# MLA scores in five single-pass products with rounded parts, and a rearranged opening

## The chip, the cores and the metric

The kernel runs on one core of a Trainium2 chip. The time is the device time of one execution, in microseconds; lower is better. The median of three runs of the kernel before is 2233.78 us (2233.66 to 2234.05).

## What is computed

Four layers on x of 512 tokens by 1024 features in float32. Layers 0 and 3 mix tokens by multi-head latent attention (MLA), layer 1 by a recurrent block, layer 2 by sliding-window attention; each layer then has a squared-ReLU MLP of width 4096, and a norm ends it. The change touches the MLA layers and the opening:

```python
def _mla(h, positions, w_in, q_norm, kv_norm, w_uq, w_ukv, w_o):
    c_q, c_kv, k_rope = jnp.split(h @ w_in, [384, 640], axis=-1)
    q = (_rmsnorm(c_q, q_norm) @ w_uq).reshape(B, S, 8, 128 + 64)
    q_nope, q_rope = q[..., :128], _rope(q[..., 128:], positions, 64)
    kv = (_rmsnorm(c_kv, kv_norm) @ w_ukv).reshape(B, S, 8, 128 + 128)
    k_nope, v = kv[..., :128], kv[..., 128:]
    k_rope = _rope(k_rope[:, :, None, :], positions, 64)[:, :, 0, :]
    for s0 in range(0, S, 128):       # block b of 128 queries sees 128 * (b + 1) keys
        s = (q_nope . k_nope + q_rope . k_rope) * (128 + 64) ** -0.5
        p = softmax(where(chunk_id[q] >= chunk_id[k], s, -1e30))
        o = p @ v
    return o @ w_o
```

## The kernel before

**Layout and weights.** Everything lies with features on the partitions and tokens along the free axis, in chunks of 128 features by 512 tokens. Weights stream through four slots (`w_raw`) in units of mostly 512 KB, in the order of `weight_units`. For each unit ScalarE makes the rounded high part (`w_hi`, `split`, L1622) and VectorE the rest (`w_lo`, L981). A projection is three single-pass products in the type float32r (`product`, L503 to L505): high by high, high by low, low by high. `square_group` (L511) takes four units of 512 by 512 columns into four PSUM banks. PSUM is used as four areas of two banks each; an area is claimed by TensorE and freed by its reader, by a semaphore that counts.

**Order.** Each engine has its program written out by hand, in the same order of tasks, with waits on semaphores. Nothing reorders them. SyncE issues all weight loads; a slot is reloaded when its low part has been made.

**The opening.** SyncE issues the column constants, then in turn 512 KB of x (two chunks) and a weight unit, four times. For each pair of chunks ScalarE makes the high parts of x times the norm's gain (L1639) and the squares (L1651), then the high part of the unit; VectorE follows with the low parts (L999, L981). GpSimd first computes the rotary angles of all tokens (`angles`, L2020 to L2062, some forty small operations of 128 by 128), and after them adds the squares (L2011).

**An MLA layer** (`mla`: L622 on TensorE, L1156 on VectorE, L1743 on ScalarE). Four units give the query compression and a part of the rest; before the third of them stand the two products that spread the angles (`rotary_angles`, L587, L588), of which ScalarE makes sin and cos (L1736, L1737), and before the fourth the token sums of squares (L564). Two narrow tail units follow. A norm goes through small columns: token sums, a root on ScalarE (L1665), Newton steps and a diagonal on VectorE (`norm_columns`, L1041), and a product of the diagonal with ones that spreads the scale over the partitions (L576, `spread`).

Then come two halves of four heads. A half starts with a projection stage: queries of two pairs of heads, keys and values of two pairs. VectorE multiplies nope queries (L1186), rotary queries (L1190) and keys (L1200) by their token scales out of PSUM, rotates with the help of a product with a permutation (L620, L1139 to L1142) and writes the values (L1206). Then attention takes the heads one after another: scores (two fp32 products for each block of queries, L704 with 128 rows and L706 with 64, key widths 512, 384, 256 and 128), mask (L1219), negated maximum (L1223), Exp with its sum (L1781), reciprocal and scaling of p (L1237, L1240), ten transposes (L720), their copies (ScalarE L1790, VectorE L1234), the weighted sum of values (L732), and its high and low parts (L1741, L1154). TensorE's order in a turn is scores of head i, weighted sum of head i - 2, transposes of head i - 1:

```python
for i in range(HALF_HEADS + 1):
    if i < HALF_HEADS: scores(i)
    if i >= 2: weighted(i - 2)
    if i >= 1 and (half, i) != (1, HALF_HEADS): transposes(i - 1)
```

Of the kernel before, what the change touches and what calls it, by code (L numbers as in the profile page):

```python
# [22 lines left out]
ALU = mybir.AluOpType  # L23
# [202 lines left out]
def trunk(nc, A):  # L226
# [3 lines left out]
    with ExitStack() as ctx:  # L230
# [23 lines left out]
        arena = sb("arena", [P, ARENA])  # L254

        def cut(*sizes):

            out, at = {}, 0
            for name, n in sizes:
# [6 lines left out]
        mla_m = cut(("qn", 4 * T), ("qr", 2 * T), ("kn", 4 * T), ("kr", T), ("v", 4 * T), ("rq", T), ("rkv", T),  # L266
                    ("pt", ATT), ("p", 2 * ATT))
# [19 lines left out]
        rstd2_4 = small[:, 64:68]  # L287
        diag = var
# [27 lines left out]
        x_loaded = [sem(f"x_loaded{i}") for i in range(4)]  # L316
        cols_loaded = sem("cols_loaded")
# [30 lines left out]
        o_hi_done = sem("o_hi_done")  # L348
        y_done = sem("y_done")
# [22 lines left out]
        OHI, OLO = HI[4:] + UHI[4:], LO[4:] + ULO[4:]  # L372
# [23 lines left out]
        def _(sp):  # L396
# [53 lines left out]
            for p in range(4):  # L450
# [34 lines left out]
        def _(pe):  # L485
# [24 lines left out]

            def square_group(areas, hi, lo, ready, before_unit=None):  # L511
# [3 lines left out]
                for kp in range(4):  # L515
# [63 lines left out]
            def rotary_angles(which):  # L579

                def run():
                    claim(3)
# [4 lines left out]
                    nc.tensor.matmul(bank(3, 0), pick, tab_m["wide_sin"], start=True, stop=True)  # L587
                    nc.tensor.matmul(bank(3, 1), pick, tab_m["wide_cos"], start=True, stop=True  # L588
# [33 lines left out]
            def mla(j):  # L622
                square_group((0, 1), HI, LO, h_chunks, {2: rotary_angles(0), 3: token_sums(2, ssq, 7)})
# [4 lines left out]
                for kq in range(2):  # L628
# [32 lines left out]
                def keys(a):  # L661
                    next_unit_ready()
                    claim(a)
                    wh, wl = (w.rearrange("p (k h n) -> p k h n", k=2, h=2) for w in unit())
# [20 lines left out]
                def swap(a, source, claimed=True):  # L685
                    if not claimed:
                        claim(a)
                    c.add("rows")
                    pe.wait_ge(rows_ready, c.now("rows"))
                    swap_rows(bank(a, 1), 0, source).then_inc(psum_done, 1)  # L690
                    c.add("psum_done")

                qn, kn, qr, kr, v = (mla_m[n] for n in ("qn", "kn", "qr", "kr", "v"))

                def scores(i):
                    rows = slice(ROPE * (i % 2), ROPE * (i % 2) + ROPE)
# [52 lines left out]
                for half in range(2):  # L749
# [3 lines left out]
                    if half == 0:  # L753
                        swap(2, mla_m["kr"], claimed=False)
                        token_sums(3, mla_m["rkv"], 1)()
                    queries((2, 3))
                    swap(1, chunk(mla_m["qr"], 0))
                    if half == 0:
                        spread(1, claimed=True)
                    keys(0)  # L760
                    if half == 1:
                        pe.wait_ge(area_free[4], c.at("area4"))
                    swap(3, chunk(mla_m["qr"], 1))
                    values(1)
                    keys(2)
# [190 lines left out]
        def _(dve):  # L956
# [67 lines left out]
            def norm_columns(out, a, n, inner=False, scale=1.0):  # L1024
# [13 lines left out]
                if inner:  # L1038
                    link(nc.vector.tensor_tensor(out, out, rstd4, ALU.mult))
                dve.wait_ge(const_loaded, 32)  # L1040
# [11 lines left out]
            def tables_made():  # L1052

                c.add("psum_done")
                c.add("area3")
                return c.now("area3")
# [99 lines left out]
            def mla(j, gain):  # L1156
                split(3)
                tables = tables_made()
# [18 lines left out]
                norm_columns(token_scale, 2, QL, inner=True, scale=SCALE)  # L1177
# [954 lines left out]
```

## Time and profile before

| what | us |
|---|---|
| median of three runs | 2233.78 |
| the profiled execution, its own time | 2234.83 |
| its span in the trace | 2233.1 |
| TensorE busy | 2147.3 (96%) |
| VectorE, ScalarE, GpSimd busy | 1163.4, 760.3, 180.5 |
| mean granted TensorE clock | 0.978 |

PE is TensorE, PEld its weight loads, DVE VectorE, ACT ScalarE, POOL GpSimd. The length of a matmul in the trace is that of its way through the array; matmuls overlap, and what one costs in a row of many is the distance of the starts. An fp32 product shows as two instructions (x2). A granted clock of 1.00 stands for 2.4 GHz, 0.50 for 1.2 GHz. In brackets behind an instruction is the idle time of its engine before it, and what ended that.

### The profile page before, as it was taken

How to read it: one execution, taken by the hardware profiler on the slowest of the kernel's cores; microseconds unless marked ns; L12 is line 12 of the kernel's file. 1: busy time of each engine (PE TensorE's matmuls, PEld its weight loads, DVE VectorE, ACT ScalarE, POOL GpSimd, SP SyncE). 2: the span in 40 equal slices, each digit the busy share in tenths (PEclk: the TensorE clock that was granted, in tenths of full speed). 3: DMA queues.
4: the chain of work that ended last, by engine and by line, in shares of the span. 5: the costliest groups of instructions: out<-in, count | busy, mean ns of one | idle time of the engine just before them, and what ended most of it. 6: DMA issues, size and time to landing. Idle time of an engine off the chain costs nothing.

```text
span 2233.1 us, 24820 instructions
## 1 busy us (share of the span) xinstructions
PE 2147.3 (96%) x9774; PEld 1716.7 (77%) x9774; DVE 1163.4 (52%) x1341; ACT 760.3 (34%) x1063; POOL 180.5 (8%) x199
## 2 busy tenths in 40 slices
PE   5999999999998999999997899999999999999997
PEld 4665888888876888888885788888876668888886
DVE  3653554444679654444566464344466537344444
ACT  4222432232456432232334442322342234232231
POOL 5000100000110200003110010000420001000000
PEclk8998999999999999999998899999999999999998
DMA  5200322233222322322321122322232012323221
GB/s 153 68 19 20 104 94 95 94 100 98 85 85 66 111 97 97 100 94 95 101 81 48 38 95 95 99 99 94 96 97 68 31 35 86 104 94 99 98 94 38
DMA packets 113134, 187.97 MB, mean 84 GB/s; under 512 B 14880, under 2 KB 26016, under 8 KB 113056
## 3 DMA queue, kind: packets, MB, share of 16 engines
q1 hardware_dynamic: 112720, 186.83, 26.0%
q8 instruction: 53, 0.87, 0.2%
q14 instruction: 25, 0.20, 0.0%
q10 hardware_dynamic: 336, 0.07, 0.0%
HBM read 184.78 MB, written 2.10 MB: 84 GB/s over the span
## 4 chain that ended last, share of the span: by engine, by line
PE 91%; DVE 5%; ACT 3%; POOL 1%; issue 1%; DMA 0%; ACTq 0%; DVEq 0%; POOLq 0%
PE psum L503 27%; PE psum L505 27%; PE psum L504 27%; PE psum L706 2%; PE psum L704 2%; PE psum L732 2%; PE psum L720 1%; PE psum L620 1%; ACT arena L1962 0%; PE psum L576 0%; DVE small L1529 0%; ACT w_hi L1622 0%; DMA const_sb<-in_const 0%; PE psum L880 0%; DVE w_lo L981 0%
## 5 line engine op out<-in xcount | busy, mean ns | idle before, releaser
L981 DVE TENSOR_TENSOR w_lo<-w_raw,w_hi 128x1024 fp32r<-128x1024 f32 (+1 forms) x346 | 428.2, 1243 | 821.5 <-ACT w_hi L1622 820.8
L1622 ACT ACTIVATE w_hi<-w_raw 128x1024 fp32r<-128x1024 f32 (+1 forms) x346 | 365.3, 1060 | 1087.8 <-PE psum L505 1087.7
L503 PE MATMUL psum<-h_hi,w_hi 128*128 128x512 f32 x1392 | 551.1, 396 | 17.2 <-DVE w_lo L981 17.2
L504 PE MATMUL psum<-h_lo,w_hi 128*128 128x512 f32 x1392 | 543.6, 391 | 0.0
L505 PE MATMUL psum<-h_hi,w_lo 128*128 128x512 f32 x1392 | 543.6, 390 | 0.0
L503 PE MATMUL psum<-u_hi,w_hi 128*128 128x512 f32 x1336 | 525.9, 394 | 7.5 <-ACT arena L1842 7.3
L504 PE MATMUL psum<-u_lo,w_hi 128*128 128x512 f32 x1336 | 521.8, 391 | 0.0
L505 PE MATMUL psum<-u_hi,w_lo 128*128 128x512 f32 x1336 | 521.6, 390 | 0.0
L503 PEld LDWEIGHTS psum<-h_hi,w_hi 128*128 128x128 f32 x1392 | 262.7, 189 | 75.0 <-issue 15.7
L504 PEld LDWEIGHTS psum<-h_lo,w_hi 128*128 128x128 f32 x1392 | 262.6, 189 | 57.4 <-issue 3.6
L505 PEld LDWEIGHTS psum<-h_hi,w_lo 128*128 128x128 f32 x1392 | 262.4, 188 | 55.2
L503 PEld LDWEIGHTS psum<-u_hi,w_hi 128*128 128x128 f32 x1336 | 252.1, 189 | 61.8 <-ACT arena L1842 8.1
L504 PEld LDWEIGHTS psum<-u_lo,w_hi 128*128 128x128 f32 x1336 | 252.2, 189 | 53.2 <-issue 1.4
L505 PEld LDWEIGHTS psum<-u_hi,w_lo 128*128 128x128 f32 x1336 | 251.9, 189 | 52.9
L2011 POOL TENSOR_TENSOR ssq<-ssq,sq 128x512 f32<-128x512 f32 x52 | 82.0, 1576 | 1353.5 <-ACT sq L1651 1351.2
L999 DVE SCALAR_TENSOR_TENSOR h_lo<-x,cols_sb,h_hi 128x512 fp32r<-128x512 f32 x64 | 86.7, 1406 | 10.4 <-ACT h_hi L1639 10.4
L1081 DVE TENSOR_TENSOR arena<-psum,rstd 128x1024 f32<-128x1024 f32 x64 | 78.0, 1218 | 13.8 <-PE psum L505 13.8
L1685 ACT ACTIVATE u_hi<-arena 128x1024 fp32r<-128x1024 f32 x64 | 68.0, 1062 | 34.8 <-DVE arena L1064 32.5
L1084 DVE TENSOR_TENSOR x<-x,arena 128x1024 f32<-128x1024 f32 x64 | 78.4, 1225 | 2.2
L1064 DVE TENSOR_TENSOR arena<-arena 128x1024 f32<-128x1024 f32 x64 | 76.1, 1230 | 0.0
L1068 DVE TENSOR_TENSOR u_lo<-arena,u_hi 128x1024 fp32r<-128x1024 f32 x64 | 75.9, 1228 | 0.0
L704 PE MATMUL psum<-arena 128*128 128x512 f32 (+3 forms) x128 | 56.4, 525 | 8.5 <-DVE arena L1206 5.3
(190 smaller groups left out, 1323.8 us busy)
## 6 DMA issues: line engine op xcount, KB each, us to landing
w_raw<-in_mlp_w SPq DMA_DIRECT2D x256, 512.0 KB, 3.7
w_raw<-in_mla_w_o SPq DMA_DIRECT2D x16, 512.0 KB, 3.5
w_raw<-in_lru_w_in SPq DMA_DIRECT2D x16, 512.0 KB, 3.9
w_raw<-in_swa_w_in SPq DMA_DIRECT2D x12, 512.0 KB, 3.7
w_raw<-in_mla_w_in SPq DMA_DIRECT2D x8, 512.0 KB, 4.7
w_raw<-in_mla_w_ukv SPq DMA_DIRECT2D x8, 512.0 KB, 4.5
w_raw<-in_lru_w_out SPq DMA_DIRECT2D x8, 512.0 KB, 3.4
w_raw<-in_swa_w_o SPq DMA_DIRECT2D x8, 512.0 KB, 3.4
```

What stands on the lines that cost most here:

```text
L503: nc.tensor.matmul(out, stat[0], mov[0], start=start, stop=False, skip_group_check=skip)
L504: nc.tensor.matmul(out, stat[0], mov[1], start=False, stop=False, skip_group_check=skip)
L505: return nc.tensor.matmul(out, stat[1], mov[0], start=False, stop=stop, skip_group_check=skip)
L704: nc.tensor.matmul(out, chunk(qn, i)[:, q_at], chunk(kn, i)[:, 0:keys_n], start=True, stop=False)
L981: nc.vector.tensor_tensor(w_lo[:, to], w_raw[:, to], exact(w_hi[:, to]), ALU.subtract).then_inc(w_ready, 1)
L999: nc.vector.scalar_tensor_tensor(out=LO[k], in0=chunk(x, k), scalar=col(*gain(k)), in1=exact(HI[k]), op0=ALU.mult, op1=ALU.subtract).then_ ...
L1064: nc.vector.tensor_tensor(r, r, r, ALU.mult).then_inc(squared, 1)
L1068: nc.vector.tensor_tensor(chunk(u_lo, 2 * (a + q), 2), chunk(mlp_m["relu"], 2 * q, 2), exact(chunk(u_hi, 2 * (a + q), 2)), ALU.subtract).t ...
L1081: free(nc.vector.tensor_tensor(two(chunk(mlp_m["scaled"], 2 * q, 2)), two(area(a)), twice(rstd2[:, :]), ALU.mult), a)
L1084: nc.vector.tensor_tensor(chunk(x, 2 * a, 2), chunk(x, 2 * a, 2), chunk(mlp_m["scaled"], 2 * q, 2), ALU.add).then_inc(x_ready, 1)
L1622: nc.scalar.activation(w_hi[:, to], w_raw[:, to], ACT.Copy).then_inc(w_hi_done, 1)
L2011: g.tensor_tensor(to, to, source, ALU.add).then_inc(squares_added, 1)
```

## The change

1. *Scores.* The nope queries are no longer multiplied by their token scale. ScalarE writes their high part (`query_hi`), VectorE the low part (`query_lo`). Keys are scaled into `k_wide`, then cut into high and low (`key_hi`, `key_lo`). Each rotated head is stored as 64 rows of high part and 64 rows of low part in one tile (`ROPE_Q`), and the rotary key has its high and low parts on 128 rows. A block of scores is five float32r products in place of two fp32 ones. The query's scale (`q_scale`) is applied by Exp and, for the maximum, by one small multiplication per area; its diagonal product is gone.
2. *First loads.* x and weights of the first unit come in halves of 256 KB, with semaphores of their own, and `first_unit` takes their products in the order in which the parts become ready. A small Square on ScalarE stands ahead.
3. *Squares.* Those of the opening are made by ScalarE behind each unit's high part and added by VectorE.
4. *Rotary angles.* Their products stand ahead of the last chunk of the second tail unit, in area 2; sin and cos are made after the second root. The frequency columns are loaded ahead of the positions.

```diff
 # TensorE
+            def first_unit(outs):
+                for kk in range(2):
+                    at = [slice(kk * T + m * P, kk * T + (m + 1) * P) for m in range(4)]
+                    pe.wait_ge(h_hi_done, kk + 1)
...
+                    for m in range(4):
+                        nc.tensor.matmul(outs[m], w_hi[:, at[m]], HI[kk], start=kk == 0, stop=False)
+                    pe.wait_ge(h_ready, kk + 1)
+                    for m in range(4):
+                        nc.tensor.matmul(outs[m], w_hi[:, at[m]], LO[kk], start=False, stop=False)
...
-                square_group((0, 1), HI, LO, h_chunks, {2: rotary_angles(0), 3: token_sums(2, ssq, 7)})
+                square_group((0, 1), HI, LO, h_chunks, {3: token_sums(2, ssq, 7)})
...
+                        if k == KC - 1:
+                            rotary_angles(0, 2)()
...
-                spread(2)
...
-                            nc.tensor.matmul(out, chunk(qn, i)[:, q_at], chunk(kn, i)[:, 0:keys_n],
-                                             start=True, stop=False)
-                            mm = nc.tensor.matmul(out, chunk(qr, i // 2)[rows, q_at], kr[rows, 0:keys_n],
+                            nc.tensor.matmul(out, qh, KHI[i][:, 0:keys_n], start=True, stop=False)
+                            nc.tensor.matmul(out, qh, KLO[i][:, 0:keys_n], start=False, stop=False)
+                            nc.tensor.matmul(out, ql, KHI[i][:, 0:keys_n], start=False, stop=False)
+                            nc.tensor.matmul(out, ROPE_Q[i][:, q_at], ROPE_KHI[:, 0:keys_n], start=False, stop=False)
+                            mm = nc.tensor.matmul(out, ROPE_Q[i][:, q_at], ROPE_KLO[:, 0:keys_n],
                                                   start=False, stop=True)
 # VectorE, the areas' maxima
+                                link(ins)
...
+                                nc.vector.tensor_tensor(lows, lows, q_scale[:, first:first + 2], ALU.mult
+                                                        ).then_inc(nmax_ready, 1)
 # VectorE, projection stage
-                    nope_queries(0, 0)
-                    units_passed(1)
-                    rotary_queries(0, 1)
+                    query_lo(0, 0)
...
+                        nc.vector.tensor_tensor(ROPE_KLO, k_raw, exact(ROPE_KHI), ALU.subtract)
...
                     finish(0, 1, wait=half == 1)
                     keys(0, 0)
+                    rope_lo(0)
                     finish(1, 3)
+                    key_lo(0)
                     values(0, 1)
+                    rope_lo(1)
                     keys(1, 2)
                     values(1, 3)
+                    key_lo(1)
                     split(2)
                     attention(half)
 # ScalarE, a half
-                    split(4)
...
+                    sum_ready()
+                    query_hi(0, 0)
+                    query_rope(0, 1)
                     if half == 1:
+                        head_hi(OHI[HALF_HEADS - 1])
+                    split(1)
+                    if half == 0:
...
+                        nc.scalar.activation(ROPE_KHI, k_raw, ACT.Copy).then_inc(rope_hi_done, 1)
+                        column_root()
+                    sum_ready()
+                    query_hi(1, 2)
+                    query_rope(1, 3)
+                    split(1)
...
+                    rope_hi(0)
...
+                    key_hi(0, half)
...
+                    rope_hi(1)
+                    c.add("tensor_unit")
+                    split(1)
...
+                    key_hi(1, half)
+                    c.add("tensor_unit")
+                    split(1)
                     attention(half)
```

## Rows read from the trace of the kernel before

**Rows 1.** The page, busy time of TensorE and its weight loads.

```profile
PE 2147.3 (96%) x9774; PEld 1716.7 (77%) x9774; DVE 1163.4 (52%) x1341; ACT 760.3 (34%) x1063; POOL 180.5 (8%) x199
```

**Rows 2.** Waits of PE, 0 to 170 us: engine, line, releaser, total, times, longest.

```profile
PE psum L587 <- POOL arena L2062: 11.6, 1, 11.6
...
PE psum L576 <- DVE var L1041: 0.8, 1, 0.8
```

**Rows 3.** Timeline of the opening: start, length, engine, line, operation, idle before.

```profile
6.05 1.28 ACT L1639 ACT_TABLE_LOAD   x1 [6.05 <-DMA x<-in_x]
...
12.11 0.76 PE L503 MATMUL psum<-h_hi,w_hi 128*128 128x512 f32 x1 [12.11 <-DVE w_lo L981]
...
15.58 0.40 PE L503 MATMUL psum<-h_hi,w_hi 128*128 128x512 f32 x1
...
24.22 0.39 PE L505 MATMUL psum<-h_hi,w_lo 128*128 128x512 f32 x1
```

**Rows 4.** Timeline, the angles on POOL and the matmul behind them.

```profile
21.82 1.15 POOL L2033 TENSOR_SCALAR arena<-arena 128x128 f32<-128x128 f32 x1
...
24.89 0.30 POOL L2033 TENSOR_SCALAR arena<-arena 128x128 f32<-128x128 f32 x1
...
36.26 1.19 PE L587 MATMUL psum<-arena,const_sb 128*128 128x512 f32 x1 [11.65 <-POOL arena L2062]
```

**Rows 5.** Windows: stretch, length, busy per engine, granted clock (PEclk), DMA.

```profile
36.30:42.30 6.00, 6.00 (x10) 3.41 (x11) 0.00 (x0) 0.00 (x0) 5.69 (x5) 0.50 0.00 0
```

**Rows 6.** Timeline of PE, a head of MLA layer 2 and the end of its half.

```profile
1739.36 1.02 PE L704 MATMUL psum<-arena 128*128 128x512 f32 x2
...
1744.31 0.49 PE L704 MATMUL psum<-arena 128*128 128x128 f32 x2
...
1745.14 2.42 PE L732 MATMUL psum<-arena 128*128 128x512 f32 x8
1747.40 1.25 PE L720 MATMUL psum<-const_sb,arena 128*128 128x128 f32 x10
...
1752.73 0.48 PE L503 MATMUL psum<-u_hi,w_hi 128*128 128x512 f32 x1
```

**Rows 7.** Timeline of PE, two single-pass matmuls of 256 columns.

```profile
1771.99 0.28 PE L505 MATMUL psum<-w_hi,u_lo 128*128 128x256 f32 x1
1772.11 0.28 PE L503 MATMUL psum<-w_hi,u_hi 128*128 128x256 f32 x1
```

**Rows 8.** Timeline of DVE and ACT, the same head.

```profile
1743.42 1.16 DVE L1223 TENSOR_REDUCE small<-psum 128x1 f32<-128x512 f32 x2
...
1744.62 0.69 ACT L1781 ACTIVATE arena<-psum,small 128x512 f32<-128x512 f32 x1 [4.46 <-DVE small L1223]
...
1747.60 0.60 ACT L1741 ACTIVATE h_hi<-psum 128x512 fp32r<-128x512 f32 x1 [0.52 <-PE psum L732]
...
1749.51 1.27 DVE L1240 TENSOR_SCALAR arena<-arena,small 128x128 f32<-128x128 f32 x4
```

**Rows 9.** Timeline of DVE and PE, end of a projection stage, start of attention.

```profile
1712.32 1.22 DVE L1200 TENSOR_TENSOR arena<-psum,arena 128x1024 f32<-128x1024 f32 x1 [0.55 <-PE psum L505]
...
1715.18 1.23 DVE L1206 TENSOR_TENSOR arena<-psum,small 128x1024 f32<-128x1024 f32 x1 [1.65 <-PE psum L505]
...
1716.33 2.35 DVE L981 TENSOR_TENSOR w_lo<-w_raw,w_hi 128x1024 fp32r<-128x1024 f32 x2
...
1716.46 1.12 PE L704 MATMUL psum<-arena 128*128 128x512 f32 x2 [1.32 <-DVE arena L1206]
```

**Rows 10.** Windows of attention in layer 1, layer 2 and the sliding-window layer.

```profile
90.00:103.70 13.70, 11.66 (x53) 7.38 (x52) 8.94 (x15) 4.71 (x7) 0.00 (x0) 1.00 0.23 77
103.70:117.40 13.70, 13.62 (x27) 6.52 (x28) 4.09 (x16) 3.96 (x14) 0.00 (x0) 0.50 0.00 1
1714.80:1728.40 13.60, 11.48 (x32) 4.43 (x32) 8.31 (x20) 4.59 (x10) 0.00 (x0) 1.00 0.24 77
1233.50:1240.30 6.80, 5.79 (x72) 4.94 (x72) 3.99 (x8) 3.68 (x18) 0.00 (x0) 0.50 0.01 2
```

More of the change, by code:

```diff
@@ L287, in trunk @@
         rstd2_4 = small[:, 64:68]
+        q_scale = small[:, 88:92]
         diag = var
@@ L514, in square_group @@
                 outs = [bank(areas[0], 0), bank(areas[0], 1), bank(areas[1], 0), bank(areas[1], 1)]
-                for kp in range(4):
+                begun = c.now("tensor_unit") == 0
+                if begun:
+                    claim(areas[1])
+                    first_unit(outs)
+                for kp in range(begun, 4):
                     if before_unit and kp in before_unit:
@@ L659, in queries, with keys @@
                     c.add("tensor_unit")
-                def keys(a):
+                def keys(a, half):
                     next_unit_ready()
                     claim(a)
+                    jobs["keys", j, half, a // 2] = c.now(f"area{a}")
                     wh, wl = (w.rearrange("p (k h n) -> p k h n", k=2, h=2) for w in unit())
@@ L1631, in units_passed, with gained, first_squares, prepare @@
                 act.wait_ge(unit_done, c.at("tensor_unit"))
-            def prepare(p, gain, ready, first=False):
+            def gained(k, gain):
+                nc.scalar.activation(HI[k], chunk(x, k), ACT.Copy, scale=col(*gain(k))).then_inc(h_hi_done, 1)
+            def first_squares(p):
+                for k in (2 * p, 2 * p + 1):
+                    nc.scalar.activation(chunk(arena, k) if k else ssq[:, :], chunk(x, k), ACT.Square
+                                         ).then_inc(squares, 1)
+            def prepare(p, gain, ready):
                 ready(p)
@@ L1638, in prepare @@
                     for k in pair:
-                        nc.scalar.activation(HI[k], chunk(x, k), ACT.Copy, scale=col(*gain(k))).then_inc(h_hi_done, 1)
+                        gained(k, gain)
                 for k in pair:
@@ L1979, in gate_jobs @@
                 return jobs["gates", a] + k
-            act.wait_ge(ones_set, 1)
-            for p in range(4):
-                def ready(p):
-                    act.wait_ge(x_loaded[p], 16)
-                prepare(p, gains(-1), ready, first=True)
+            act.wait_ge(x0_loaded, 16)
+            gained(0, gains(-1))
+            act.wait_ge(w0_loaded, 16)
+            nc.scalar.activation(w_hi[:, 0:T], w_raw[:, 0:T], ACT.Copy).then_inc(w0_hi_done, 1)
+            act.wait_ge(x_loaded[0], 16)
+            gained(1, gains(-1))
+            c.add("loaded0", 16)
+            act.wait_ge(w_loaded[0], c.now("loaded0"))
+            nc.scalar.activation(w_hi[:, T:PAIR], w_raw[:, T:PAIR], ACT.Copy).then_inc(w_hi_done, 1)
+            c.add("unit")
+            for p in range(1, 4):
+                act.wait_ge(x_loaded[p], 16)
+                gained(2 * p, gains(-1))
+                gained(2 * p + 1, gains(-1))
                 split(1)
+                first_squares(p - 1)
+            first_squares(3)
+            c.add("squares_added", 7)
             for n, (kind, i) in enumerate(PHASES):
@@ L2070, in _ @@
             angles(0)
-            squares_of_x(first=True)
+            c.add("squares", KC)
+            c.add("added", KC - 1)
             for n, (kind, i) in enumerate(PHASES):
```

227 lines of the change are left out of this document (167 added, 60 removed).

## The prediction

> **What bounds the kernel now.** I read the page first: TensorE is busy for 96% of the span [rows 1], so time can only come from work that it no longer does, from a place where it stands still, or from a stretch at the lower of its two clocks. The waits of TensorE over the first layer then name the places. It stands 11.6 us on GpSimd's rotary angles and 0.8 us on a diagonal [rows 2]. In the opening the first x lands at 6.05 us, a table load follows it, and the first matmul starts at 12.11 us, when the first low weight half is there [rows 3]. The second stand ends only when the long chain of small GpSimd operations is through, at 36.26 us, and the granted clock is then 0.50, that is 1.2 GHz [rows 4, 5]. In attention TensorE hardly waits: one head runs from its first score product to its transposes without a hole [rows 6]. So there the multiplications themselves are the bound, with VectorE behind them by little [rows 8].
>
> **The sum's base.** The profiled execution took 2234.83 us (span 2233.1, 1.7 us around it), 1.05 us over the median of 2233.78. I take differences from the trace and set them against the median.
>
> **The opening.** x and the first weights come as halves of 256 KB, each followed by its own hi and lo step; a small activation in front draws the table load under the transfers. Before, 512 KB of x landed at 6.05 us after other traffic. With half of it I expect landing near 5.2, the high half of x at 5.9, that of the weights at 6.5, and the first matmul there, 5.6 us earlier than 12.11. The bounds: landing at 4.3 would gain 6.5 us, the old landing with half-width steps behind it 4.7; if the second half unit then comes late, 3. The steps on TensorE stay 24 per unit; 38 of them took from 15.58 to 24.22, so 0.227 us each [rows 3].
>
> The angles' two products move from ahead of the third unit to ahead of the last eighth of the narrow tail units. TensorE then reaches them at 6.5 + 6.9 (first unit: 24 x 0.227 and 1.4 for its slow start, since the nine steps from 12.11 to 15.58 took 3.47 us and not 2.05) + 72 x 0.227 + 0.8 (token sums) + 1.1 (diagonal) + 5.5 + 0.8 + 4.1 (18 steps) = 42.1 us. GpSimd is ready at 36.3 now. It starts perhaps 1 us earlier, since its frequency transfer is issued first. But seven additions of 512 columns move from GpSimd to VectorE, and the same kind of GpSimd step took 1.15 us beside a busy VectorE and 0.30 beside an idle one [rows 4]; at worst the seven cost it 7 x 0.61 = 4.3 us (half the 1.22 of a 1024-column step in [rows 9]). It is ready between 35 and 40, ahead of 42.1, and the 11.65 us stand goes. With it goes the stretch at 1.2 GHz up to 42.3 us, six microseconds at half pace, so 3.0 us [rows 5]. The sums of squares on VectorE are done before unit four, since ScalarE's squares come right behind each pair; now GpSimd's nine microseconds of additions merely follow the angles.
>
> The tables leave ScalarE's way to the first root (a load and two Sin, 2.6 us), so the 0.77 us wait at the diagonal goes, and one of two diagonal products goes entirely (1.07 us), because the query scale is now applied inside Exp. Opening: 5.6 + 11.65 + 3.0 + 0.77 + 1.07 = 22.1 us, bounds 16 (x late by 2.6, the angles by 3.5) and 23. The second MLA layer has no stand on angles; it gains the last two, 1.8 us.
>
> **The products of the scores.** Now a head has eight fp32 products (a 128-row and a 64-row one for each of four widths), 5.78 us from 1739.36 to 1745.14 [rows 6]. Afterwards there are twenty single-pass ones. Those of 512 columns cost 0.227 us, of 256 columns 0.12 (successive starts in [rows 7]), of 384 by interpolation 0.173. For 128 columns the trace has none; the nearest is the ten transposes of 128 columns, starting at 1747.40 [rows 6] and ending about 1.1 us later, 0.11 each. Bounds are 0.06 (in proportion to width) and 0.21 (half the 0.42 of an fp32 product of 128 columns, 1744.31 to 1744.72 with its start). I take 0.11. A head is 5 x (0.227 + 0.173 + 0.12 + 0.11) = 3.15 us, so TensorE has 2.63 us less work, 42 us over 16 heads.
>
> **What becomes late instead.** A turn of three tasks on TensorE falls from 9.1 to 3.15 + 2.3 (weighted sums) + 1.1 = 6.5 us. The other engines have a cycle of their own: VectorE masks and reduces (1.38 us to the end of the 1.16 row), plus a link and a new small multiplication (0.2); ScalarE does eight Exp pieces, 1744.62 to 1747.08 (0.52 before 1747.60), 2.35 without a short wait; then ScalarE takes the head's high half, VectorE its low half, the copy, the reciprocal and the scaling of p, 1747.60 to 1750.78, 3.18 [rows 8]. That is 7.1 us, and VectorE then begins the next head. So the period is 7.1, not 6.5. At the start of a half VectorE comes to head 0 only 3.6 us after TensorE: the low half of keys 2 and 3 (1.15) now stands before the two weight halves (2.35) [rows 9]. Exp of the first area ends 3.0 us later, and TensorE, done at 3.15, begins head 1 at 6.6. p of head 1 is ready at 14.3, of heads 2 and 3 at 21.5 and 28.7; the third weighted sum starts at 27.3 and the last transposes end at 30.7. The old half took from 1716.46 [rows 9] to 1752.73 [rows 6], 36.3. Gain 5.6 us in each of four halves, 22.4, little more than half of 42.
>
> **The projection stages pay.** High halves go to ScalarE (some 1.1 us per pair of heads, beside TensorE). On VectorE the scaling of nope queries and keys is replaced one for one by a subtraction or kept, two rotary multiplications go (2 x 0.62), and there are added, before scores start, four subtractions for rotated queries (4 x 0.62), one low half of keys (1.15) and in half 0 that of the rotary key (0.62). So VectorE has 3.0 us more in half 0 and 2.4 in half 1. It had idle time of 0.55 + 1.65 us at the end of the stage [rows 9], and TensorE waits for its last value copy already. In half 0 ScalarE's third root comes 1.5 us later, behind a copy and a table load, since Sin stands between. I get the start of scores 2.35 us later in half 0 and 1.0 in half 1, 6.7 us over both layers. Bounds: nothing if ScalarE and VectorE overlap better, and 2 x (3.0 + 1.5 + 2.4) = 13.8 with no idle time to fill.
> The Trainium skill ("ScalarE: Activation LUTs", Table sets) says that each set has one expensive function and that going from one to another costs a load, about 2.7 us. The loads in this trace took 1.28 [rows 3]; by the page's figure the stage would be 1.4 us later per layer.
>
> **The clock.** Both halves of layer 1 had one stretch of 13.7 us at 0.50 with TensorE busy for 13.62 of it; the stretch before it had been busy for 11.66 of 13.7. Layer 2, busy for 11.48 of 13.6, stayed at full clock [rows 10]. Each low stretch cost about 6.8 us, 13.6 in all. In the new loop the holes are longer: some 3 us before each half, 3.4 us behind head 0, and 1 to 2 us later. I expect the clock to fall in all four halves. How long it stays low I can bound only: the sliding-window layer has stretches of 6.8 us at 0.50 between busier ones [rows 10], the old MLA 13.7. While low, scores take 6.3 us and the 7.1 us cycle turns into one of 13, but part of the loss falls into holes: for 13.7 us my schedule gives 5.1 us, for 6.8 us about 2.5. The new products are dense single-pass ones, like those under which the clock came back in the opening (0.50 up to 42.3 us, [rows 5]), so I take the shorter: 4 x 2.5 = 10 us.
> The Trainium skill ("TensorE: Matmul & The Clock Gate", A second HAM failure mode) warns that micro-idles between groups of matmuls which cycle PSUM make the clock oscillate. Layer 1 bears it out, layer 2 does not.
>
> **Sum.** 22.1 + 1.8 + 22.4 - 6.7 + 13.6 - 10 = 43.2 us, so 2233.8 - 43.2 = 2190.6, about 2191.
>
> **Rivals.**
> - *The clock stays up through attention.* Nothing of the 10 us is paid: 2181. For it: layer 2 at 1.00 with 2 us of holes. Against it: the new holes are longer. Chance 0.2.
> - *The clock falls as before in every half* for 13.7 us: 20.4 instead of 10, so 2201; an opening that gains only 12 us (angles late through VectorE's additions, x no earlier) gives the same time. For it: the second line of [rows 10] and the 1.15 us row in [rows 4]. Chance 0.2.
> - *The products are the whole bound*, VectorE finding room: 42 instead of 22.4, so 2171. Against it the cycle of 7.1 us, each part of which has a row. Chance 0.06.
> - *Slower: the holes keep TensorE at 1.2 GHz through attention.* Then 23.9 us of work per half becomes 47.8 instead of 30.7, 17 us in each of four halves. With no low clock the sum is 53; three halves wholly low turn it into nothing, four give 2233.8 - 53 + 68 = 2249. Chance 0.03, as no stretch in attention stayed low over 13.7 us.
> The forecast has the remaining 0.51.
>
> **From these to the numbers.** A measurement of this kernel can tell about 0.2%, 4.5 us, from no change. Faster by more: 0.51 + 0.2 + 0.2 + 0.06 less a margin of 0.01, 0.96; within it 0.01; slower 0.03. The range takes the first two rivals whole and the bounds of opening and stages around the forecast: 2177 to 2208.
>
> **What would show it.** The first matmul near 6.5 us; no wait on POOL at the angles, and TensorE past them near 42; the first queries of layer 1 some 22 us earlier, near 45.6; 0.11 us for the narrow products; a period of about 7.1 us with TensorE waiting on the pt copies in the last turns; four short stretches at 0.50. I am wrong if a period is near 6.5 or above 8, if the stage before scores grows by over 3 us in half 1, or if the angles hold TensorE.

## The result

The changed kernel takes 2201.15 us (median of 4 runs, 2197.62 to 2204.94) beside 2233.72 us of the kernel before on the same chip (2225.48 to 2234.05): ratio 0.9883, interval 0.9855 to 0.9912. The forecast was 2191, range 2177 to 2208. The profiled execution took 2204.94 us (span 2203.2) against the 2234.83 of the profile before, 29.9 us less. The tables below split these 29.9 us.

On the page after, TensorE is as full as it was [rows 1], with less work; VectorE has 24 us more and ScalarE 37:

```profile
PE 2111.5 (96%) x9834; PEld 1737.6 (79%) x9834; DVE 1187.8 (54%) x1395; ACT 796.9 (36%) x1108; POOL 175.9 (8%) x192
```

The waits of TensorE up to 205 us (line waiting, releaser, total, times, longest) are of another kind than [rows 2]. The angles are gone from the list. The score products (L765) now wait for Exp (L1942) and for a copy of values (L1293), the weighted sums (L795) for VectorE's copy (L1325), and the token sums of the query compression (L615) for GpSimd's additions of squares (L2206), which nothing in the forecast priced:

```profile
PE psum L765 <- ACT arena L1942: 6.6, 4, 2.2
PE psum L545 <- ACT w_hi L2167: 6.3, 1, 6.3
PE psum L765 <- DVE arena L1293: 6.0, 2, 3.4
PE psum L795 <- DVE arena L1325: 4.6, 2, 2.3
PE psum L615 <- POOL arena L2206: 3.7, 1, 3.7
```

**The opening after**, timeline of TensorE. First matmul at 6.29 us instead of 12.11 [rows 3]; the first token sums at 24.33 (46.41 before); the second ones stand for 3.71 us; the angles' products at 49.19 wait for nothing; the first query product starts at 52.30. I set it against 67.64 of before, the second one there, since the first, at 67.00, runs slowly behind the diagonal (a shift of 0.23 us at most between the first two rows of the table):

```profile
6.29 2.05 PE L545 MATMUL psum<-h_hi,w_hi 128*128 128x512 f32 x4 [6.29 <-ACT w_hi L2167]
...
24.33 0.83 PE L615 MATMUL psum<-ones,ssq 128*128 128x1 f32 x6
...
41.31 1.84 PE L615 MATMUL psum<-ones,arena 128*128 128x1 f32 x8 [3.71 <-POOL arena L2206]
...
49.19 1.02 PE L638 MATMUL psum<-arena,const_sb 128*128 128x512 f32 x2
...
52.30 0.39 PE L527 MATMUL psum<-u_hi,w_hi 128*128 128x512 f32 x1
```

GpSimd meanwhile, which has the additions directly behind the angles (L2257), and the windows of TensorE behind the stand (stretch, length, busy, granted clock, DMA). 6.8 us run at 1.2 GHz, of which TensorE works for the last 5.9, from 41.3 us:

```profile
36.57 2.04 POOL L2257 TENSOR_TENSOR arena<-arena,const_sb 128x512 f32<-128x512 f32 x2
38.57 2.60 POOL L2206 TENSOR_TENSOR arena<-arena,sq 128x512 f32<-128x512 f32 x2
```

```profile
24.30:40.40 16.10, 13.25 (x59) 1.00 0.56 150
40.40:47.20 6.80, 5.88 (x18) 0.50 0.00 0
```

**A head of attention after** (layer 1, TensorE). Products of 256 columns start 0.12 us apart, those of 128 columns 0.11; the head takes 98.86 to 102.07, 3.21 us, where the old one took 5.78 [rows 6]:

```profile
101.21 0.28 PE L767 MATMUL psum<-h_hi,arena_r 128*128 128x256 f32 x1
101.33 0.28 PE L768 MATMUL psum<-u_lo,u_hi 128*128 128x256 f32 x1
...
101.73 0.28 PE L767 MATMUL psum<-h_hi,arena_r 128*128 128x128 f32 x1
101.84 0.27 PE L768 MATMUL psum<-u_lo,u_hi 128*128 128x128 f32 x1
```

VectorE's turn, here in layer 2, is memset to memset, 1707.16 to 1714.35, 7.19 us. It waits 2.02 us for the high half of an earlier head's output, which itself stands behind the Exp pieces in ScalarE's queue; TensorE's third weighted sum then waits 2.31 us for the copy (L1325). The turn before it, in which no output is cut into high and low, took 5.63 us (1701.53 to 1707.16):

```profile
1707.16 0.19 DVE L1306 MEMSET psum<- 64x64 f32 x2
...
1711.79 0.69 DVE L1219 TENSOR_TENSOR h_lo<-psum,h_hi 128x512 fp32r<-128x512 f32 x1 [2.02 <-ACT h_hi L1879]
1712.40 0.55 DVE L1325 COPY arena<-psum 128x384 f32<-128x384 f32 x1
...
1714.35 0.19 DVE L1306 MEMSET psum<- 64x64 f32 x2
```

```profile
1691.55 0.50 PE L765 MATMUL psum<-h_hi,arena_r 128*128 128x512 f32 x1 [3.38 <-DVE arena L1293]
...
1720.24 2.40 PE L795 MATMUL psum<-arena 128*128 128x512 f32 x8 [2.31 <-DVE arena L1325]
```

**The clock in attention.** Before, layer 1 had two stretches of 13.7 us at 1.2 GHz, one in each half. The first is in [rows 10]; this is the second, in a window set by eye, so that it takes in a little of the full clock:

```profile
175.80:189.50 13.70, 13.70 (x28) 0.52 0.00 1
```

After, each half has two or three of 3.4 us (0.51 of the full clock, that is 1.2 GHz), each behind a stand; here those of half 0 of layer 1, windows of TensorE:

```profile
77.00:84.00 7.00, 4.22 (x30) 1.00 0.00 0
84.70:88.10 3.40, 3.40 (x10) 0.51 0.03 10
88.10:91.50 3.40, 1.47 (x12) 0.99 0.77 270
91.50:95.00 3.50, 3.27 (x9) 0.51 0.09 33
```

**Where the 29.9 us lie**, from the starts in the two traces (before, after). The forecast's column has its own terms, with 6.8 us of old low clock and 2.5 of new in each half of layer 1, and 2.5 of new in layer 2. A positive gain is time saved. The ends of the stretches are the query product above, first scores (S) and third weighted sums (W) of each half, and layer 2's token sums (T).

| stretch | before, us | after, us | gained | forecast |
|---|---|---|---|---|
| start to queries | 67.64 | 52.30 | 15.3 | 22.1 |
| to S, half 0 | 29.4 | 32.3 | -2.9 | -2.35 |
| S to W, half 0 | 39.3 | 29.7 | 9.6 | 9.9 |
| W to S, half 1 | 32.2 | 35.3 | -3.0 | -1.0 |
| S to W, half 1 | 39.4 | 29.7 | 9.7 | 9.9 |
| to T of layer 2 | 1457.8 | 1459.2 | -1.3 | 0 |
| T to S, layer 2 | 50.6 | 53.1 | -2.5 | -0.55 |
| S to W, half 0 | 33.0 | 28.7 | 4.3 | 3.1 |
| W to S, half 1 | 32.2 | 33.6 | -1.3 | -1.0 |
| S to W, half 1 | 33.0 | 29.7 | 3.3 | 3.1 |
| to the end | | | -1.3 | 0 |
| sum | | | 29.9 | 43.2 |

### The profile page after: what moved, and what is told of

The parts are those of the page before. It is cut to its first block, busy times and chain, and to the rows that moved or that the text cites. A ratio compares the mean times of both kernels' runs of the same rounds, so it can differ in the third digit from the quotient of the medians.

```text
span 2203.2 us, 25037 instructions
## 1 busy us (share of the span) xinstructions
PE 2111.5 (96%) x9834; PEld 1737.6 (79%) x9834; DVE 1187.8 (54%) x1395; ACT 796.9 (36%) x1108; POOL 175.9 (8%) x192
## 4 chain that ended last, share of the span: by engine, by line
PE 84%; DVE 9%; ACT 4%; POOL 1%; issue 1%; DMA 0%; ACTq 0%; DVEq 0%; POOLq 0%
PE psum L527 27%; PE psum L528 27%; PE psum L529 27%; ACT arena L1942 2%; PE psum L795 1%; DVE small L1310 1%; DVE w_lo L1044 1%; DVE arena L1331 0%; PE psum L943 0%; ACT arena L2145 0%; DVE small L1629 0%; PE psum L765 0%; ACT w_hi L1752 0%; PE psum L671 0%; DVE arena L1467 0%
## 5 line engine op out<-in xcount | busy, mean ns | idle before, releaser
L2206 POOL TENSOR_TENSOR ssq<-ssq,sq 128x512 f32<-128x512 f32 x52 | 82.0, 1577 | 1339.4 <-ACT sq L1789 1337.1
L1818 ACT ACTIVATE arena<-psum 128x1024 f32<-128x1024 f32 x64 | 61.5, 1012 | 0.0
```

Source lines behind the costliest of these rows:

```text
L2206: g.tensor_tensor(to, to, source, ALU.add).then_inc(squares_added, 1)
```

## The experiments

Twelve kernels, in three batches; two of the twelve are unedited. The kernel before lay at 2225.83 (15 runs), 2225.34 (11) and 2225.41 us (23) in them, always between 2219 and 2236. Where an experiment is an edit of the changed kernel, it is set against the control's 2204.46. The control ran in the first batch alone, and the third batch (before_again, before_filled, late, best3) ran on another chip than the first two; the fastest times of the kernel before on the two chips, 2218.86 and 2218.95 us, agree. The ratios are taken against the kernel before of the same batch. Several experiments are also compared by places of their traces, with S, W and T as in the table; a trace is one execution.

**control**: the changed kernel, unedited.

> The changed kernel again, unedited, as the base for the other three on the same chip. Every theory expects 2197 to 2205 us and the same holes on TensorE: 3.7 us for GpSimd in the opening, 3.4 and 2.7 us ahead of the two halves of attention, some 1.7 to 2.2 us behind head 0.

2204.46 us (2199.93 to 2205.09, 6 runs), ratio 0.9887 (0.986 to 0.9914). The same stands with the same lengths as above, and the stretches at 1.2 GHz in attention at the same places within 2 us, one in the opening shorter.

**q_sums**: the three additions of query squares of layer 1 go from GpSimd's queue to VectorE, between its low halves.

```
+ def query_squares(made, added, to, source):
+     if j == 0:
+         dve.wait_ge(squares, made); dve.wait_ge(squares_added, added)
+         nc.vector.tensor_tensor(to, to, source, ALU.add).then_inc(squares_added, 1)
```

> In the first MLA layer VectorE adds the squares of the compressed queries and keys, in place of GpSimd, whose queue has them behind the rotary angles. Theory A (the opening lost its missing 7 us there): the wait of 3.7 us at the query's token sums goes, and with it the stretch at 1.2 GHz behind it, 3.1 us; some 7 us faster than the control, near 2194. Rival (TensorE would stop at the next thing anyway, the angles' own products or VectorE's low halves, which now come later): under 2 us faster, with a new wait at the angles or at a unit's low part.

2198.84 us (2197.56 to 2201.55, 6), ratio 0.9868 (0.9841 to 0.9895): 5.6 us under the control. The stand at the token sums is 1.8 us instead of the control's 3.7, and is now on VectorE's L1240. The queries of layer 1 start at 49.45 us instead of 51.92, so 2.5 us of the gain lie where the theory put them. The other 3 come later, where the clock falls at other places. In the MLA layers that evens out (no low stretch at 114 us, one more in layer 2). From the last W of layer 1 to T of layer 2 it does not: 1456.1 us for the control's 1459.2. What moved the clock there I can't say. GpSimd's queue was a cause of the stand, VectorE's additions are the next one, and the 7 us of the theory held in size only by what came behind.

```profile
PE psum L615 <- DVE arena L1240: 1.8, 1, 1.8
```

**filled**: idle single-pass products of 512 columns in TensorE's stands: 12 (10 in half 1) ahead of a half, 13 behind head 0, 4 behind head 1, 9 ahead of the last weighted sums. Their results are overwritten.

```
+ def fill(n, a=0):
+     pe.wait_ge(area_free[a], c.now(f"area{a}"))
+     for _ in range(n):
+         nc.tensor.matmul(bank(a), UHI[4][:, 0:P], UHI[4], start=True, stop=True)
```

> TensorE does products that nobody reads while it would wait: 12 or 10 of 512 columns ahead of a half's attention, 13 behind head 0, 4 behind the first transposes, 9 ahead of the last turn. The results are unchanged. Theory B (the holes make the clock fall, and that costs time in attention and behind it): no stretch at 1.2 GHz in the MLA halves, 8 to 12 us faster than the control, near 2191. Rival (the chain of VectorE and ScalarE sets the pace, and a slow TensorE hides behind it): the clock stays up and the time changes by under 3 us.

2194.72 us (2191.16 to 2195.41, 5), ratio 0.9845 (0.9815 to 0.9875): 9.7 us less, for TensorE doing some 150 products more. No stretch at 1.2 GHz is left in either MLA layer's attention:

```profile
77.00:84.00 7.00, 6.36 (x39) 1.00 0.00 0
84.00:91.00 7.00, 6.82 (x36) 1.00 0.46 150
91.00:98.00 7.00, 5.88 (x38) 1.00 0.01 2
98.00:105.00 7.00, 7.00 (x43) 1.00 0.00 0
```

This prices the clock, but not by itself. S to W is 28.66 us in all four halves now, where it was 28.7 to 29.7; W to S in layer 1 is 33.6 instead of 35.3. The two profiled executions are 12.4 us apart (2204.52 and 2192.12). Of these, 3.1 lie between S and W, 1.7 in the stage of layer 1 and 3.3 behind W in the second halves, 8.1 in the MLA layers together. Another 0.8 us lies in the opening, and 4.1 in the layers between, which the edit does not touch: TensorE has the same 6611 products there, and what differs is the granted clock. These windows reach from the fourth weighted sum of layer 1's second half to T of layer 2 (stretch, length, busy, granted clock, DMA), the control's first:

```profile
194.84:1638.08 1443.24, 1408.27 (x6611) 0.98 0.28 90
```

```profile
188.66:1627.76 1439.10, 1402.82 (x6611) 0.99 0.28 91
```

So the new low clock of the MLA layers cost about 8 us by the traces, where the forecast had 10, and only 3 of it between S and W, where the forecast put all.

**scores_only**: the old opening (512 KB loads, angles ahead of the third unit, tables ahead of the first root) with the new scores. The opening's squares stay on VectorE, and the early table load and the order of the frequency columns stay as changed.

> The new scores and projection stages with the old opening: loads of 512 KB, first unit as any other, angles ahead of the third unit and tables ahead of the first root in both MLA layers. The squares of the opening stay on VectorE. By the two traces the opening brought 22.1 us up to the first token sums and gave 6.8 of it back by the start of the queries. Theory: the scores' part alone is 16 to 20 us faster than the kernel before, 2214 to 2218, and the opening is worth the other 14 to 17. Rival (the two parts share a gain, since an earlier start only shifts where the clock falls): 2205 to 2210.

2217.32 us (2214.79 to 2217.76, 10), ratio 0.9952 (0.9933 to 0.997). Against the control, what was taken back is worth 12.9 us. Against the kernel before the scores are worth only 8.5, not 16 to 20; the last batch bears on that.

**rotary_back**: only the angles' products and the tables go back to their old places.

```
-                  {3: token_sums(2, ssq, 7)})
+                  {2: rotary_angles(0), 3: token_sums(2, ssq, 7)})
```

> The changed kernel with the angles' products ahead of the third unit again, and sin and cos ahead of the first root. TensorE comes to them near 18.9 us and GpSimd is ready near 38: a hole of 19 us, of which the 3.7 us at the query sums are given back. Theory (each part of the opening gets its full time): 14 to 18 us slower than the changed kernel, 2215 to 2219. Rival (TensorE catches up later, as GpSimd and VectorE have been done by then): under 8 us slower.

2215.66 us (2213.8 to 2217.26, 6), ratio 0.9948 (0.9929 to 0.9968): 11.2 us more than the control, between the two theories. TensorE, begun 6 us earlier, stands 17.0 us for the angles instead of 11.6 [rows 2], the diagonal's 0.8 is back, and the 3.7 us for the query squares is gone, as they are done by then. An earlier start without this move would have been worth less than 2 us (scores_only 2217.32): the first matmul at 6.29 would only have waited longer.

```profile
PE psum L638 <- POOL arena L2255: 17.0, 1, 17.0
...
PE psum L627 <- DVE var L1104: 0.8, 1, 0.8
```

**three_of_five**: two of the five products of each score block are left out (q high by k low, q low by k high), so the scores are less exact. 20 us of work less on TensorE.

```
- nc.tensor.matmul(out, qh, KLO[i][:, 0:keys_n], start=False, stop=False)
- nc.tensor.matmul(out, ql, KHI[i][:, 0:keys_n], start=False, stop=False)
```

> Two of the five products of a block of scores are left out (high query by low key, low query by high key); scores are less exact. TensorE has 1.3 us less work a head, 20 us in all. Theory C (the chain of VectorE and ScalarE is the bound): at most 4 us faster than the changed kernel, since only the first product of an area stands in the chain (0.8 us for head 0 of a half), and perhaps slower, as the holes grow and the clock falls more; 2197 to 2203. Rival (the products are the bound): 15 to 20 us faster, 2182 to 2186.

2199.36 us (2196.72 to 2200.41, 5), ratio 0.9873 (0.9851 to 0.9895): 5 us for 20 (at most 4 were expected). The first two rows are the waits of TensorE in this kernel over the whole span, the two in the second fence those of the changed kernel. Most of the work taken away turns into standing: these two kinds of wait grow from 21.5 to 34.1 us. The cycle over ScalarE and VectorE is the bound in attention, as forecast.

```profile
PE psum L793 <- DVE arena L1323: 17.1, 8, 3.7
PE psum L765 <- ACT arena L1940: 17.0, 8, 4.5
```

```profile
PE psum L765 <- ACT arena L1942: 12.2, 8, 2.2
...
PE psum L795 <- DVE arena L1325: 9.3, 4, 2.3
```

**reorder**: VectorE does the copy, the reciprocal and the scaling of p ahead of the head's low half, so that it does not wait 2 us for the high half.

> Only VectorE's order within a head of MLA attention changes: the copy of the transposes, the reciprocal and the scaling of p come ahead of the low half of an earlier head's output, which waits for ScalarE. Theory C (the bound of attention is the chain reduction, Exp, high half, low half, copy, scaling, reduction, 7.2 us a turn): the turn falls to TensorE's 6.5 us, 1 to 2 us a half, 4 to 7 us in all, near 2196. Rival (TensorE's own work and clock set the time): no change, under 1 us.

2202.69 us (2198.25 to 2206.48, 6), ratio 0.9893 (0.9871 to 0.9915), 1.8 us less and inside the runs' spread: my theory's size failed. The low half frees the bank in which the next weighted sum is built, and that now comes last:

```profile
1715.49 4.05 PE L795 MATMUL psum<-arena 128*128 128x512 f32 x8 [2.73 <-DVE h_lo L1219]
```

**best2**: q_sums, filled and reorder together.

> The query sums on VectorE, the filled holes and VectorE's new order together. If theories A, B and C hold and their gains add: 7 + 10 + 5 us under the changed kernel, near 2179. Fillers longer than a hole would cost up to 0.2 us each; if the clock did not matter, near 2189.

2190.88 us (2188.56 to 2192.8, 5), ratio 0.9837 (0.9815 to 0.9859). The first two alone add up to 2189.2 (2204.46 - 5.6 - 9.7), so reorder gave nothing more, and the 2179 of the three theories together is missed by 12. No stretch at 1.2 GHz is left in the MLA layers of this trace, and S to W is 29.1 us in all four halves where filled has 28.7: at full clock VectorE's new order is a little slower.

**before_again**: the kernel before, unedited, profiled a second time.

> The kernel before, unedited, for a second profile of it. Its times so far lie in clusters (about 2219, 2225, 2230, 2234 us) while its instructions are always the same. My theory: the clusters differ by how many stretches of 13.7 us at 1.2 GHz fall into the MLA layers (the first profile had two in attention and one in the opening, and each costs about half its length, 6.8 us). So a profile of some 2220 should show none or one of them in attention, with every other duration unchanged, and one of 2227 one. Rival: the spread comes from elsewhere (transfers, the recurrent or the sliding-window layer), then the two stretches of layer 1 are there again whatever the time.

2231.72 us (2218.95 to 2235.58, 12), ratio 1.0004 (0.9979 to 1.0029). This profiled execution took 2229.71 us (span 2227.9), 5.1 less than the first. Its stands are the same (1.32 us ahead of the half, 0.80 behind head 0), but the stretch at 104 us that was at 0.50 in [rows 10] is at full clock here, and there is one long stretch, in half 1 of layer 1. That is the theory's one stretch for a run of some 2227, but it is 20.4 us long and not 13.7:

```profile
104.00:117.70 13.70, 13.70 (x47) 1.00 0.00 1
160.00:163.00 3.00, 1.69 (x4) 1.00 0.02 5
163.00:183.40 20.40, 20.40 (x40) 0.51 0.17 52
```

**before_filled**: the kernel before with five idle products ahead of each half and three behind head 0.

> The kernel before, with five idle single-pass products put into the 1.3 us stand of TensorE ahead of each half of attention, and three into the 0.8 us stand behind head 0 (their results are overwritten). My theory: these two short stands are what let the clock fall in attention now and then; filled, no long low stretch is left there, and all runs lie together at the fast end of the kernel before, 2218 to 2222, ratio to the kernel before about 0.997 with hardly any spread. The long low stretches that the forecast counted as 13.6 us given back would then be a matter of which run of before one looks at. Rival: the clock falls for the amount of work (11.7 of 13.7 us busy) and not for the stands; then the extra products change nothing or make it fall as often, and the time is 2225 to 2235 with the same spread.

2220.51 us (2217.66 to 2222.34, 12), ratio 0.9966 (0.9947 to 0.9984). The spread of 17 us becomes 5, at the lower end, though TensorE does 32 products more. The granted clock stays at 1.00 through the start of attention; no stretch at 1.2 GHz is left in either MLA layer behind the opening:

```profile
94.60:101.40 6.80, 6.65 (x20) 1.00 0.47 148
101.40:108.00 6.60, 6.60 (x19) 1.00 0.03 8
```

So the kernel before had 27.4 us at 1.2 GHz in attention in one execution and 20.4 in another. S to W tells what that cost: in layer 1 it is 39.3 and 39.4 us in the first trace, 33.0 and 41.6 in the second, 33.0 and 33.0 here. The 27.4 us cost 12.7 and the 20.4 cost 8.6, a little under half. The rest of the difference between the three profiled executions (2234.83, 2229.71, 2222.04) lies mainly in the opening, which is 1.7 and 0.7 us longer than here up to the first query product, and in the layers between, which are 1.4 us shorter. Only these three traces were looked at; that the runs at 2219 had no low stretch is inferred. Two things stay open. The products fill the stands and also give TensorE more work, so this run does not tell the stands from the amount of work as the cause. And layer 2 has the same stands and stayed at full clock in all three traces.

**late**: of what VectorE does between its last keys and head 0, the last copy of values, the low half of keys 2 and 3 and a weight half go behind head 0's reductions, another weight half behind head 1's. For that the wide keys 2 and 3 pass through the room of the transposed weights, ScalarE makes one high half of weights behind head 0's Exp, and TensorE no longer waits for the last copy of values.

```
-                    values(1, 3); key_lo(1); split(2)       # before attention(half)
+                        if i == 0: values(1, 3); key_lo(1); split(1)
+                        if i == 1: split(1)
```

> The changed kernel, with what VectorE does between its last keys and head 0 moved behind head 0: the last copy of values, the low half of keys 2 and 3 and one weight half (3.6 us) go behind head 0's reductions, the second weight half (1.2 us) behind head 1's; one high half of weights on ScalarE goes behind head 0's Exp; the keys pass through the room of the transposed weights. TensorE no longer waits for the last copy of values. My theory: VectorE's work ahead of scores is what each half pays (3.4 and 2.7 us of stand on TensorE), and behind head 0 there is idle time for it (1.5 us under the Exp). p of head 0 is ready about 3 us earlier, 2.5 to 3 us stay in each of four halves: 2192 to 2195, 10 to 12 us under the changed kernel (2204). Rival, after the reordering inside the turn that gave only 1.8 of 4 to 7 us: the work is only moved to where the turn of 7.1 us is just as bound, and what comes off ahead of head 0 comes back behind it: under 4 us, 2200 to 2204.

2186.06 us (2184.44 to 2189.51, 6), ratio 0.9817 (0.979 to 0.9843): 18.4 us under the control, which ran on the other chip (by the two ratios 0.0070, some 16 us, each ratio with an interval of 6 us to either side); more than the 10 to 12 of the theory and the opposite of its rival. VectorE comes from the last wide keys (L1281) straight to head 0, and fills the time under Exp:

```profile
1676.08 1.23 DVE L1281 TENSOR_TENSOR arena<-psum,arena 128x1024 f32<-128x1024 f32 x1
1677.30 0.18 DVE L1307 MEMSET psum<- 64x64 f32 x2
...
1679.83 1.22 DVE L1294 TENSOR_TENSOR arena<-psum,small 128x1024 f32<-128x1024 f32 x1
1680.96 1.22 DVE L1287 TENSOR_TENSOR h_lo<-arena,h_hi 128x1024 fp32r<-128x1024 f32 x1
1682.10 1.22 DVE L1044 TENSOR_TENSOR w_lo<-w_raw,w_hi 128x1024 fp32r<-128x1024 f32 x1
1683.23 0.17 DVE L1335 RECIPROCAL small<-small 128x4 f32<-128x4 f32 x1
```

From that L1281 to the reciprocal of head 0 it is 7.15 us here; in the changed kernel (1689.14 to 1699.17 for the same steps) 10.0. That is the 3 us of the theory, 12 over four halves. The traces of late and control, 18.2 us apart, say where the rest lies. The stages ahead of S are 12.9 us shorter in all (12.8 between best3 and filled, whose stages are free of low clock), S to W 1.9, the way from the last W of layer 1 to T 3.3 and the end 1.1, and the start of the queries is 0.9 later. The 5 us outside the stages go with less time at 1.2 GHz: attention has six low stretches, one of them 6.8 us, instead of eleven, and between the last W of layer 1 and T there are 37.5 us of it instead of 51.2. No run isolated that.

**best3**: late, q_sums and the idle products behind head 0, behind head 1 and ahead of the last weighted sums.

> The same move, with VectorE's additions of the query squares and with the idle products that keep the clock up (12 behind head 0, 4 behind head 1, 9 ahead of the last weighted sums of a half; none ahead of the half, where no stand should be left). The two earlier edits together should be worth 15.3 us by their own runs. Theory: with the 10 to 12 us of the move 2176 to 2180. The rival of the move gives 2186 to 2189. If the parts overlap (the move shortens stands that the idle products also covered), 2181 to 2185.

2185.23 us (2183.35 to 2185.28, 6), ratio 0.9809 (0.9783 to 0.9835), the fastest kernel here, but no faster than late alone by more than the spread. The parts do not add. By the traces the gain of q_sums is there (the first query product starts 3.5 us earlier than in late), but S to W is 5.9 us longer over the four halves, with less low clock in it: the idle products now take time of their own. The four products behind head 1 now come after the wait for Exp, that is after the stand instead of in it:

```profile
151.06 2.08 PE L757 MATMUL psum<-u_hi 128*128 128x512 f32 x4 [1.82 <-ACT arena L1969]
```

late with q_sums and without idle products was not run.

## Why the prediction was right, and where its steps were not

The direction and the range were right. The sum was 13.3 us too high against the profile (29.9 for 43.2): 6.8 in the opening, 4.8 in the stages, 2.7 outside both, less 1.0 that S to W gave more. The median came out 10 us above the forecast. Of the signs named beforehand, the first matmul, the widths' costs and the waits came as said; the queries of layer 1 start at 52.30 us and not near 45.6, and the stage into half 1 of layer 1 grew by 3.0 us, at the limit that the prediction itself set.

- **First matmul and start.** Forecast near 6.5 us, found 6.29; the gain up to the first token sums is 22.1 us (46.41 to 24.33), of which the forecast had 5.6 + 11.65 + 3.0 = 20.25. Right; most of the 1.8 more is the time of the angles' two products, which now stand behind the sums.
- **The second token sums, entered as 0.8 us without a wait.** This is the step that failed. I checked the angles against TensorE's new time (42.1) and not GpSimd's additions of the query squares, which are queued behind the angles and for which TensorE waits at the second token sums, ahead of the angles' products. The prediction's own terms put TensorE there at 37.1 us (found 37.6) and GpSimd's angles at 35 to 40 (found 38.6), so a stand could have been read from them. (The sentence on GpSimd's nine microseconds of additions is on the seven for x in the kernel before, which the change gives to VectorE.) The stand is 3.7 us, and from 41.3 to 47.2 TensorE works at half pace, 2.9 us of loss. Together 6.6, against the 6.8 that the opening lacks. (The angles' products cost this part some 1.7 us, which the part before them gained.) q_sums shows that the queue is part of it: half of the stand and 2.5 us of the opening come back.
- **Products.** 0.11, 0.12, 0.175 and 3.21 us a head for 0.11, 0.12, 0.173 and 3.15. Right; the upper bound of 0.21 and the lower of 0.06 were not needed.
- **The turn bound by ScalarE and VectorE.** 7.19 us for 7.1 in the turn in which an output is cut, with the TensorE wait on the copy that was forecast; the turn before it takes 5.63, which the schedule had at 7.1 too. three_of_five confirms it: the rival in which products are the whole bound is out.
- **Length of a half.** 27.3 us at full clock was forecast, 28.66 found in filled. With 1.0 instead of 2.5 us of low clock inside it the two errors cancel (29.7 for 29.8), which is luck: at full clock the new loop is worth 17.5 us over four halves (33.03 less 28.66 each), not 22.4. I did not isolate the 1.4 us; the four idle products behind head 1 may be part of it.
- **Stages.** At full clock the stage into half 1 grew by 1.3 us (forecast 1.0), in layer 1 by 3.0, since one low stretch falls into it. Half 0 grew by 2.9 and, in layer 2, by 2.5 net of the tables' gain (forecast 0.55), so about 2 us too few. The kind was right, VectorE's added work ahead of scores; late shows that this work, with what stood there already, could have been hidden under Exp.
- **The new low clock.** In all four halves, in short stretches: right in kind. There are eleven of 3.4 us and not four of 6.8. That filled's 9.7 us is so near the 10 of the forecast is in part luck: by the traces 8.1 us lie in the MLA layers and 3.1 where the forecast put them. The first two stretches of a half follow the stands ahead of the half and behind head 0.
  The Trainium skill ("TensorE: Matmul & The Clock Gate", A second HAM failure mode: psum-queue depth-cycling) says that small idles between groups of matmuls can make the clock go up and down. filled and before_filled agree: with the stands filled, attention stays at 2.4 GHz in both traces.
- **The old low clock, 13.6 us "given back".** Right for the profile on which I based the sum (12.7 by S to W), but not a property of the kernel before: it depends on the run. The base of 2233.78 was such a run too; over more runs the kernel before lies at 2225.4 to 2225.8. Against before_filled (2220.5), without long stretches in attention, the change is worth 16 to 19 us; by places 15.3 in the opening and 14.4 between S and W (4 x 33.03 less 117.7), less 9.8 in the stages and 2.7 elsewhere, 17.2. This goes with the small gain of scores_only: 8.5 against a median of 2225.8, and 3.2 against before_filled, which ran on the other chip.

## What to carry to other kernels

When a wait is moved away, list everything queued behind the slow engine's work and ask for each piece who waits for it at the new time; the second in the queue becomes the stand. A faster matrix stage hands the bound to a cycle over two other engines, and then the place to win is at its start: put work that only later heads need under the first Exp. Before counting a slow-clock stretch of one profile as a gain, profile the kernel a second time, or fill the stands of TensorE and see what the time becomes.

## What the hardware showed that I had not expected

A stand of 1.3 us with another of 0.8 us behind it is followed, in some executions and not in others, by 13.7 to 20.4 us at 1.2 GHz in otherwise full work; eight idle products per half end it (17 us of spread to 5). In the changed kernel longer stands (3.4 and 1.7 us) are followed by stretches of 3.4 us only. Some 150 matmuls more made the kernel 9.7 us faster. And the clock differs in layers that an edit does not touch: for the same 6611 products between the MLA layers the control takes 1443.2 us, with 47.8 at 1.2 GHz, q_sums 1440.1 and filled 1439.1, with 37.5 each. So a difference of 3 us between two edits can come from there alone. Whether the edit or the execution moves it is open: the two traces of the changed kernel agree, and each edit has only one.
